# Half of a window attention's probability turning moved from TensorE to VectorE and DRAM, and the weights' high parts taken ahead of the attention's slots

## The reference, cut to what matters

```python
s = einsum('bnqhgd,bnkhd->bhgnqk', qc, kb) * HEAD_DIM ** -0.5     # kb: own chunk and two before
s = where(valid, s, -1e30)
m = maximum(max(s, -1), sink)
p = exp(s - m)
denom = sum(p, -1) + exp(sink - m)
o = einsum('bhgnqk,bnkhd->bnqhgd', p / denom, vb)
a = (o * silu(za)) @ w_att_out
```

## Time and profile before

| | |
|---|---|
| median of 3 executions | 1270.36 us (1270.28 to 1270.67) |
| the profiled execution | 1270.71 us, span of its instructions 1268.9 us |
| granted TensorE clock, mean | 0.999 |
| TensorE busy | 1261.5 us, 99% of the span |
| VectorE / ScalarE / GpSimd busy | 893.3 / 619.7 / 724.1 us |
| slots 0 to 18 | about 818 to 906 us of the span |

### The profile page before, as it was taken

How to read it: one execution, slowest core, us unless ns; L and a number is a source line. 1 busy time by engine, 2 the same in 40 slices (tenths; PEclk the granted TensorE clock), 3 DMA queues, 4 the chain that set the end, 5 groups by cost and what they waited for, 6 DMA issues and landing times.

```text
span 1268.9 us, 19753 instructions
## 1 busy us (share of the span) xinstructions
PE 1261.5 (99%) x7542; PEld 1091.2 (86%) x7542; DVE 893.3 (70%) x1380; ACT 619.7 (49%) x989; POOL 724.1 (57%) x513
## 2 busy tenths in 40 slices
PE   9999999999999999999999999999999999999998
PEld 7877877777888899989988998877778899999886
DVE  6775555777444599558855869766656999998587
ACT  6123533565334555325522546354556656666454
POOL 3543433434543588658865866444333786666767
PEclk9999999999999999999999999999999999999999
DMA  7253176564423335353535335333522233225351
GB/s 225 87 150 108 42 199 159 144 187 125 124 75 100 100 100 166 100 166 100 167 101 166 103 106 174 108 88 88 137 67 68 76 121 100 89 83 199 100 210 73
DMA packets 205371, 154.89 MB, mean 122 GB/s; under 512 B 67488, under 2 KB 194976, under 8 KB 204512
## 3 DMA queue, kind: packets, MB, share of 16 engines
q1 hardware_dynamic: 204800, 153.06, 40.3%
q10 hardware_dynamic: 480, 0.59, 0.1%
HBM read 136.20 MB, written 14.16 MB: 118 GB/s over the span
## 4 chain that ended last, share of the span: by engine, by line
PE 96%; ACT 1%; DVE 1%; DMA 1%; POOL 1%; issue 0%; SPq 0%; ACTq 0%
PE gemm L961 16%; PE gemm L962 16%; PE gemm L969 16%; PE gemm L1235 10%; PE gemm L1234 10%; PE gemm L1239 10%; PE gemm L985 2%; PE gemm L986 2%; PE gemm L991 2%; PE gemm L1018 2%; PE gemm L1019 2%; PE gemm L1024 2%; PE mix L1355 1%; PE mix L1343 1%; PE mix L1332 1%; DMA raw<-w_in 1%
## 5 line engine op out<-in xcount | busy, mean ns | idle before, releaser
L793 POOL TENSOR_TENSOR wlo<-raw,whi 128x512 fp32r<-128x512 f32 x264 | 368.7, 1428 | 288.6 <-ACT whi L1491 269.1
L961 PE MATMUL gemm<-hh,whi 128*128 128x512 f32 x544 | 215.3, 396 | 0.2 <-ACT whi L1491 0.2
L962 PE MATMUL gemm<-hl,whi 128*128 128x512 f32 x544 | 212.4, 390 | 0.0
L813 POOL TENSOR_TENSOR wlo<-raw,whi 128x512 fp32r<-128x512 f32 x108 | 159.4, 1501 | 40.5 <-ACT whi L1685 32.4
L1491 ACT ACTIVATE whi<-raw 128x2048 fp32r<-128x2048 f32 x62 | 118.4, 1909 | 46.0 <-PE gemm L969 19.8
L969 PE MATMUL gemm<-hh,wlo 128*128 128x512 f32 x544 | 136.0, 391 | 0.0
L1234 PE MATMUL gemm<-hh,whi 128*128 128x256 f32 x496 | 124.8, 284 | 0.0
L961 PEld LDWEIGHTS gemm<-hh,whi 128*128 128x128 f32 x544 | 102.1, 188 | 26.3 <-issue 4.3
L1235 PE MATMUL gemm<-hl,whi 128*128 128x256 f32 x496 | 124.4, 284 | 0.0
L962 PEld LDWEIGHTS gemm<-hl,whi 128*128 128x128 f32 x544 | 102.3, 188 | 20.4
L969 PEld LDWEIGHTS gemm<-hh,wlo 128*128 128x128 f32 x544 | 101.7, 188 | 20.9
(11 more groups left out here) (545 smaller groups left out, 3124.6 us busy)
## 6 DMA issues: line engine op xcount, KB each, us to landing
raw<-w_in SPq DMA_DIRECT2D x53, 1024.0 KB, 5.3
raw<-w_gu SPq DMA_DIRECT2D x44, 512.0 KB, 5.2
raw<-w_down SPq DMA_DIRECT2D x16, 512.0 KB, 4.4
p_rows<-p_blocks SPq DMA_DIRECT2D x32, 160.0 KB, 3.2
p_t<-p_rows SPq DMA_DIRECT2D x8, 640.0 KB, 4.0
raw<-w_o SPq DMA_DIRECT2D x5, 1024.0 KB, 5.2
raw_b<-w_branch SPq DMA_DIRECT2D x16, 256.0 KB, 6.8
blk_b<-w_o SPq DMA_DIRECT2D x8, 512.0 KB, 7.1
```

The costliest lines, as they stand in the source:

```text
L793: last = nc.gpsimd.tensor_tensor(a(wlo), a(raw), as_f32(a(whi)), ALU.subtract)
L813: return nc.gpsimd.tensor_tensor(part_of(wlo, u, b), raw_block(u, f, k), as_f32(part_of(whi, u, b)), sub)
L961: mm(bank[:, :], w, xh[:, k, :], start=(k == 0), stop=False)
L962: mm(bank[:, :], w, xl[:, k, :], start=False, stop=False)
```

## The change

For the first 16 steps (v below 8) the turning leaves TensorE. VectorE transposes the 32x32 blocks of both steps (`w_blockwise`) directly behind the scaling; SyncE stores them with four DMAs of 128 KB to DRAM (`w_rows`) and loads them with one of 512 KB (`w_turned_p`); TensorE multiplies both steps with the values in slot 2v+5, and reads its moving operand as four segments of 32 columns. The turns of 16 steps and their copies on ScalarE go. The last 16 steps stay as they were. ScalarE's `split` for the next unit stands ahead of the slots of a tile, not behind them. SyncE's order in this stretch is written anew; the layer norm's vectors are loaded later, and VectorE waits for them where it first uses one. In the first block's attention a store's wait stands ahead of the stores. VectorE clears the parts of the block tile that no step writes.

```diff
+w_blocks = [place(f"w_blocks{i}", [P, 1024], Z0 + at) for i, at in enumerate((80, 98))]
+w_turned_p = [place(f"w_turned_p{i}", [P, 1024], Z0 + 68 + 4 * i) for i in range(2)]
...
+BY_DMA = 8
+S_PE = 2 * BY_DMA
...
+w_rows = nc.dram_tensor("w_rows", (2, P, 1024), f32, kind="Internal").ap()
...
         sp.wait_ge(sem("p_turned"), i + 1)
-        for f in range(4):
-            sp.dma_start(p_rows[i % 2].rearrange("(j a) (k c) -> a k j c", a=32, c=P)[:, :, :, 32 * f:32 * f + 32],
-                         p_blocks[32 * f:32 * f + 32, :].rearrange("a (k j b) -> a k j b", j=4, b=32)).then_inc(sem("p_stored"), 16)
         if 2 <= i < HEADS + 2:
...
             sp.wait_ge(sem("st_o"), i - HEADS - 1)
+        for f in range(4):
+            sp.dma_start(p_rows[i % 2].rearrange("(j a) (k c) -> a k j c", a=32, c=P)[:, :, :, 32 * f:32 * f + 32],
+                         p_blocks[32 * f:32 * f + 32, :].rearrange("a (k j b) -> a k j b", j=4, b=32)).then_inc(sem("p_stored"), 16)
         sp.wait_ge(sem("p_stored"), 64 * (i + 1))
...
         sp.dma_start(cs2[:, :, :], cst2a.rearrange("p (a s) -> p a s", a=2)).then_inc(sem("c2_in"), 16)
-        sp.dma_start(lng[:, :], ln_g.partition_broadcast(P)).then_inc(sem("c2_in"), 16)
         stream(n0 + part + 2, 2, down_from(2 * UC))
-        sp.wait_ge(sem("tile_free"), tiles_before(n0 + part))
-        sp.dma_start(lnb[:, :], ln_b.partition_broadcast(P)).then_inc(sem("c2_in"), 16)
-        sp.dma_start(bsb[:, :, :].rearrange("p g i -> p (g i)"), sg_b.partition_broadcast(P)).then_inc(sem("c2_in"), 16)
     slot_free(n_e0)
...
+    def store_probs(v):
+        sp.wait_ge(sem("w_tb"), v + 1)
+        if v >= 2:
+            sp.wait_ge(sem("w_v"), 2 * v - 2)
+        for f in range(4):
+            sp.dma_start(w_rows[v % 2].rearrange("(j a) c -> a j c", a=32)[:, :, 256 * f:256 * f + 256],
+                         w_blocks[v % 2][32 * f:32 * f + 32, :].rearrange("a (j c) -> a j c", j=4)).then_inc(sem("w_stored"), 16)
+    def load_probs(v):
+        sp.wait_ge(sem("w_stored"), 64 * (v + 1))
+        sp.dma_start(w_turned_p[v % 2][:, :], w_rows[v % 2]).then_inc(sem("w_in"), 16)
...
+    load_qz(n_qz + 2)
+    swap_rotary(0)
+    load_qz(n_qz + 3)
+    load_qz(n_qz + 4)
+    store_probs(0)
+    swap_rotary(1)
+    load_probs(0)
+    store_turned(0)
+    store_probs(1)
+    load_qz(n_qz + 5)
+    load_probs(1)
+    store_turned(1)
+    store_probs(2)
+    load_qz(n_qz + 6)
+    load_probs(2)
+    store_probs(3)
+    load_probs(3)
+    swap_rotary(2)
+    store_turned(2)
+    store_probs(4)
+    load_qz(n_qz + 7)
+    load_probs(4)
+    store_turned(3)
+    store_probs(5)
     load_wide(0)
+    load_probs(5)
+    store_probs(6)
+    load_probs(6)
     swap_rotary(3)
+    load_wide(1)
     store_turned(4)
+    store_probs(7)
+    load_probs(7)
+    store_turned(5)
+    load_wide(2)
+    store_turned(6)
+    load_wide(3)
+    store_turned(7)
...
+    sp.wait_ge(sem("w_v"), S_PE)
+    sp.dma_start(lng[:, :], ln_g.partition_broadcast(P)).then_inc(sem("c2_in"), 16)
+    sp.dma_start(lnb[:, :], ln_b.partition_broadcast(P)).then_inc(sem("c2_in"), 16)
+    sp.dma_start(bsb[:, :, :].rearrange("p g i -> p (g i)"), sg_b.partition_broadcast(P)).then_inc(sem("c2_in"), 16)
...
         m, c = s // TT, s % TT
         pe.wait_ge(sem("w_p"), s + 1)
-        if s >= 1:
-            pe.wait_ge(sem("w_pt"), s)
+        if s > S_PE:
+            pe.wait_ge(sem("w_pt"), s - S_PE)
         for h in range(2):
             for kb_ in keys_of(c):
...
         m, c = s // TT, s % TT
-        pe.wait_ge(sem("w_pt"), s + 1)
+        if s < S_PE:
+            pe.wait_ge(sem("w_in"), 16 * (s // 2 + 1))
+            by_block = w_turned_p[s // 2 % 2].rearrange("p (f k b) -> p k f b", k=8, b=32)
+            turned = lambda k: by_block[:, s % 2 * 4 + k]
+        else:
+            pe.wait_ge(sem("w_pt"), s - S_PE + 1)
+            turned = lambda k: wpt[:, s % 2, k * P:(k + 1) * P]
         if c == 0 and m >= 1:
...
                 last = mm(M[3][64 * h:64 * h + 64, c * P:(c + 1) * P], v2[:, c - 1 + kb_, kv * DH:(kv + 1) * DH],
-                          wpt[:, s % 2, (2 * h + kb_) * P:(2 * h + kb_ + 1) * P],
+                          turned(2 * h + kb_),
                           start=(kb_ == keys_of(c)[0]), stop=(kb_ == 1))
...
                 w_scores(i // 2)
-            for s in (i - 4, i - 3):
-                if 0 <= s < STEPS:
-                    w_values(s)
-        if 0 <= i - 2 < STEPS:
+        first = i - 4 if i % 2 == 0 else i - 5
+        if (S_PE <= first < STEPS) if i % 2 == 0 else (0 <= first < S_PE):
+            w_values(first)
+            w_values(first + 1)
+        if S_PE <= i - 2 < STEPS:
             w_turn(i - 2)
...
             s = 2 * v + e
-            if s >= 3:
-                act.wait_ge(sem("w_t"), s - 2)
+            if s >= S_PE + 3:
+                act.wait_ge(sem("w_t"), s - 2 - S_PE)
+            elif s >= 3:
+                act.wait_ge(sem("w_tb"), (s - 3) // 2 + 1)
             for h in range(2):
...
     def w_turned(s):
-        act.wait_ge(sem("w_t"), s + 1)
-        if s >= 2:
+        act.wait_ge(sem("w_t"), s + 1 - S_PE)
+        if s >= S_PE + 2:
             act.wait_ge(sem("w_v"), s - 1)
...
         i = pos[0]
-        if 0 <= i - 2 < STEPS:
+        if S_PE <= i - 2 < STEPS:
             w_turned(i - 2)
...
         for u in range(2):
             for j in range(2):
+                if j == 0 and p + u > 0:
+                    split(n + u + 1)
                 for _ in W_AT[2 * u + j] if p else ():
                     w_slot()
-                if j == 0 and p + u > 0:
-                    split(n + u + 1)
                 if u == 1 and j == 1:
                     attention_gate(2 * p)
...
     T = tiles_before(n_e0)
-    dve.wait_ge(sem("c2_in"), 64)
+    dve.wait_ge(sem("c2_in"), 16)
     tile_ready(T)
...
     def attention_consts():
+        for h in range(2):
+            v.memset(w_blocks[0].rearrange("p (j k b) -> p k j b", j=4, b=32)[:, 2 * h], 0.0)
         v.memset(w_score[0:64, :, :, 192:256], NEG)
...
+    def w_blockwise(v_):
+        dve.wait_ge(sem("w_p"), 2 * v_ + 2)
+        if v_ >= 2:
+            dve.wait_ge(sem("w_stored"), 64 * (v_ - 1))
+        blocks = w_blocks[v_ % 2].rearrange("p (j k b) -> p k j b", j=4, b=32)
+        for s in (2 * v_, 2 * v_ + 1):
+            probs = wp[:, s % 3].rearrange("p h (k j b) -> p (h k) j b", j=4, b=32)
+            own = blocks[:, s % 2 * 4:s % 2 * 4 + 4]
+            if s % TT == 0:
+                for k in (1, 3):
+                    last = v.transpose(own[:, k], probs[:, k])
+            else:
+                last = v.transpose(own, probs)
+        last.then_inc(sem("w_tb"), 1)
     def w_out(m):
...
                 w_norm(i // 2)
+            if i < S_PE:
+                w_blockwise(i // 2)
         if i % TT == 3 and i >= 7:
...
         dve.wait_ge(sem("ln_rs"), 1)
+        dve.wait_ge(sem("c2_in"), 64)
         link(stt(out=vg[:, t, :], in0=vg[:, t, :], scalar=ln_neg[:, t:t + 1], in1=lng[:, :], op0=ALU.add, op1=ALU.mult))
```

More of the change, by code:

```diff
@@ L719, in store_turned @@
                                  x_turned[m % 4][32 * f:32 * f + 32, :].rearrange("a (j b) -> a j b", b=32)).then_inc(sem("x_stored"), 16)
[L721 to L734, removed]
@@ L735, in _ @@
-            slot_free(n_vs)
+            def store_probs(v):
[8 more added lines that the diff above has]
+                sp.dma_start(w_turned_p[v % 2][:, :], w_rows[v % 2]).then_inc(sem("w_in"), 16)
@@ L736, in load_wide, with load_qz @@
+            def load_qz(n):
+                slot_free(n)
+                p, j = divmod(n - n_qz, 2)
+                load(n, cols(w_in2, (I2_ZA if j else I2_Q) + p * UC, UC))
             def load_wide(u):
+                slot_free(n_vs + u)
                 slot = raw[:, (n_vs + u) % 2].rearrange("p (k a) c -> p k (a c)", a=2)
                 load(n_vs + u, cols(w_in2, I2_VS + u // 2 * 512, 512, 4 * (u % 2), 4), slot)
+            load_qz(n_qz)
+            load_qz(n_qz + 1)
+            sp.wait_ge(sem("key_s"), 1)
@@ new lines, in _ @@
+            for a, b in ((0, 8), (8, 0)):
+                for kv in range(2):
+                    sp.dma_start(key_t[a:a + 8, kv, :], key_s[64 * kv + b:64 * kv + b + 8, :]).then_inc(sem("key_in"), 16)
+            load_qz(n_qz + 2)
[9 more added lines that the diff above has]
+            load_probs(1)
@@ L742, in _ @@
             store_turned(4)
+            store_probs(7)
[5 more added lines that the diff above has]
+            store_turned(7)
+            slot_free(n_ao)
+            load(n_ao, cols(w_ao, 0, UC))
+            sp.wait_ge(sem("w_v"), S_PE)
+            sp.dma_start(lng[:, :], ln_g.partition_broadcast(P)).then_inc(sem("c2_in"), 16)
+            sp.dma_start(lnb[:, :], ln_b.partition_broadcast(P)).then_inc(sem("c2_in"), 16)
@@ L743, in _ @@
+            sp.dma_start(bsb[:, :, :].rearrange("p g i -> p (g i)"), sg_b.partition_broadcast(P)).then_inc(sem("c2_in"), 16)
```

(2 more changed lines are left out.)

## The result

The changed kernel takes 1272.68 us (median of 20 executions, 1271.51 to 1274.55) where the kernel before takes 1270.43 (20 executions, 1270.25 to 1271.68): the ratio is 1.0018, 95% interval 1.0012 to 1.0025, some 2.2 us slower. The forecast was 1273.4. The profiled execution took 1273.55 us, 2.84 more than the profiled one of before.

The account below looks back on a forecast made before the run. TensorE, busy 1261.5 of 1268.9 us, was taken to bound the kernel: 1270.71 less 4.2 saving plus 7.2 waits gave 1273.7, with the median 0.35 lower 1273.4; range 1266.5 to 1276.8, likeliest case 1271.6 to 1275.4.

Parts of the forecast that it names:

- The saving: TensorE's visits in slots 2 to 19 fall from 22.74 to 18.53 us, saving 4.2 us.
- The walk: Slots 8 to 20: VectorE's operations followed in time beside GpSimd's, giving TensorE waits of 7.2 us in all.
- The mechanism: VectorE, late from 9.2 us more transposes, waits for GpSimd and TensorE for VectorE; 5.5 to 9 us of waits, chance 0.46.
- the seven places: TensorE waits: scores(6) 1.6, scores buffer after soft(7) 0.3, values(6) 2.2, scores(9) 0.7, first turn 0.4, scores(10) 0.4, values(8) 1.6.
- the scaling of pair 6: Slots 12 to 16: norm(6) falls into GpSimd's work and waits twice, 1.2 us each.
- soft(9): Slots 16 to 20: it meets the next split's GpSimd work, making scores(10) 0.4 us late.
- (1): VectorE stays in time beside GpSimd: 1266.2 if no collision hurts; chance in full 0.24, half the waits 0.16.
- (2): Blocks come late through SyncE's queue, TensorE waits at odd slots: 1276.4; chance 0.14 for rivals 2 to 4 together.
- (3): Values' four-segment operand costs +0.067 us per instruction, +7.5: 1276 to 1281; chance 0.14 for rivals 2 to 4 together.
- (4): VectorE's strided transposes slower than 0.65, at 0.85 2.9 us more: 1276; chance 0.14 for rivals 2 to 4 together.
- The sentence on the port: VectorE and GpSimd share a port pair as exclusive lock; the loser blocks for the whole instruction, 1.25 us per two-input VectorE operation.

Follow-up runs that it names:

- twelve pairs: First 12 pairs of steps turned by VectorE and DRAM instead of 8, GpSimd held back: 1271.34 us; with SyncE's order mended and n_vs+2 held too, 1264.29 us.
- the second profile: The changed kernel profiled once more, with nothing changed: one execution, 1271.49 us.
- the run with few blocks: Changed kernel with block transposes of pairs 2 to 7 left out but for one 128x128 piece per step: 1267.74 us, ratio 0.9981 to the kernel before.
- the second order: Twelve pairs, GpSimd held back, stores of pairs 8 and 9 put ahead of the weight loads of n_vs+2 and n_vs+3: 1267.23 us, ratio 0.9974.
- the third: Twelve pairs, GpSimd held back, load of n_vs+3 and two last row stores no longer before the stores of pairs 9 and 10: 1267.09 us, ratio 0.9973.

## Why the prediction was right

**The saving.** 4.2 us forecast; 4.1 measured where all waits are gone, and 6.2 against 4.2 + 2.1 with twelve pairs. The visits have the lengths that the sum gave them.

**The walk.** The mechanism, the engines and the semaphores are as forecast, and so are six of the seven places. Forecast waits 1.6, 0.3, 2.2, 0.7, 0.4, 0.4, 1.6, together 7.2; measured 0.78, 0, 1.85, 0.38, 0.41, 0.20, 1.87, together 5.5. The term that was too large is the first: I let the scaling of pair 4 end at 862.1, and it ended at 861.5; the first GpSimd instruction began 0.8 us earlier than I had it, so `atl` waited 0.5 and not 0.85. `finish_q` ended at 869.4, not 870.7. That is most of the 0.8 at scores(6); how much of what is missing later was handed on from there was not isolated. Two steps were not as walked. The scaling of pair 6 waited 1.8 us (2.84 instead of 1.01) and not twice 1.2: the earlier trace rows show 2.05 instead of 1.01, one wait of 1.0. And soft(9) did not meet GpSimd's work, it took 1.18; it was late behind the scaling of the first block's output, which did (1.55 instead of 0.74, at 907.04). An earlier meeting, at 834 (two gates 2.57, `finish_q` 2.20), was not in the walk; no wait of TensorE followed it directly.

**The clock** was not in the sum. It took 1.6 us in the profiled execution and nothing in the second profile, and it made up for the 1.7 us that the walk had too much. So the profiled execution's 1273.55 against the 1273.7 of the sum is luck: for the executions at 0.999 or 1.000, 1271.5 to 1272.65, the forecast of 1273.4 is 0.8 to 1.9 us too high. The median lies where the mechanism was given 0.46; by the forecast's own measure of 0.2% it counts as no change (0.32), though the interval of the ratio lies above 1.

**Rivals.** (1) half happened: VectorE's operations do go through back to back when it comes first, as the transposes behind the gates showed, but not in the order of the changed kernel. (2) hardly happened with eight pairs (0.2 us in one of two profiles, 0.8 with the transposes behind the gates), and did with twelve. (3) and (4) did not: values take 0.86 and 1.07, the transposes of an odd pair 1.30 (those of an even pair 1.1, not 1.0).

**The sentence on the port.** That the loser waits for the whole instruction was right in size (a gate took 1.73; the forecast had 1.25 of waiting and 0.61 of its own). That the waiting falls to VectorE each time was mine, and wrong as a rule: where VectorE was first, GpSimd waited (2.50 us). The Trainium skill, "SBUF — State Buffer", section "Who interferes with whom", has it: "Issue order, not op shape, decides who blocks." The traces agree for the first meeting: with GpSimd there first `atl` took 1.21, with `atl` there first GpSimd's instruction took 2.50. They do not agree for the two gates behind `atl`, which were issued after GpSimd's instruction (861.73) and did not wait (1.29 for both), nor for the run with few blocks, where `atl` began 0.03 us behind GpSimd's instruction (860.11 and 860.08) and took 0.65. The sum had left the order out.

## What to carry to other kernels

When work moves to an engine off the path, walk that engine's queue in time and look at whom its later operations will then meet; the price was not the 9.2 us of transposes as such. They made VectorE late, each two-input operation that fell beside GpSimd added about a microsecond, and TensorE paid for what went beyond VectorE's slack: with either of the two taken out, 4.3 us or more of the 5.5 went. An engine with slack should be told when to start: holding GpSimd back by a semaphore cost nothing and gave the change its saving. After each such repair look again for the same collision one place further on.

## What was not expected of the hardware

Beside four GpSimd subtractions that began first, VectorE's back-to-back operations alternated with them (1.21, 1.76 and 1.7 us); when VectorE was first, three operations of 0.65 each ran through and the GpSimd instruction took 2.50 us. And after a stretch with TensorE busy 1.94 of 4 us, the granted clock was 0.58 over the next 4 us in one execution and 1.00 in another of the same kernel. With twelve pairs, 1.68 of 4 us busy (the second order) and 1.23 (the third) were followed by 1.00 as well. With the split behind the slots, where TensorE was busy 0.80 of 4 us, it fell:

```profile
900.00:904.00 4.00, 0.80 (x4) 0.48 (x3) 3.67 (x6) 2.99 (x6) 4.00 (x4) 1.00 0.42 118
904.00:908.00 4.00, 4.00 (x26) 2.64 (x25) 4.00 (x4) 0.45 (x2) 4.00 (x4) 0.63 1.08 266
```

So a wait of TensorE can cost more than its own length, by a half-speed stretch behind it; here such a stretch came behind waits of 1.87, 3.2 and 4.8 us, and none behind waits of 1.86, 2.3 and 2.8. What decides is not shown.
